# A one-core decoder step: queries spread over the partitions by DMA, four PSUM banks for the products, cached pages and value quads moved, squares of two norms added up by VectorE

## What is computed

```
h = x
for i in (0, 1):
    hn = rms_norm(h, g_pre[i])
    out = gla_mixer(hn, ...) if i == 0 else sb_mixer(hn, ..., k_all, v_all, ...)
    h = h + out
    h = h + sigmoid(rms_norm(h, g_ple[i]) @ w_ple_gate[i]) * (p[i] @ w_ple_up[i])
    if i == 0:
        k_new, v_new = split(rms_norm(h, g_kv) @ w_kv)
        k_all = concat(cache_k[page_table], k_new)      # 16 pages of 128 positions for each sample
        v_all = concat(cache_v[page_table], v_new)
return rms_norm(h, g_final), states, k_new, v_new
# stick breaking: A[t,s] = sigmoid(z_ts) * prod_{s<j<t} (1 - sigmoid(z_tj)), z = q.k/sqrt(64) + bias_h
```

## Time and profile before

| | |
|---|---|
| runs | 950.82, 952.33, 953.08 us, median 952.33 |
| profiled execution | 954.14 us, span 951.2 us between its first and last instruction |
| busy in the span | PE 892.9, DVE 549.9, ACT 439.4, POOL 293.6 us |
| moved by DMA | 228.26 MB, 240 GB/s over the span |

### The profile page before, as it was taken

The page is one execution under the profiler, slowest core; times in us unless marked ns, Lnnn a source line. Parts: engine busy times, 40 slices in busy tenths (PEclk is TensorE's granted clock), DMA queues, the critical chain, the costliest instruction groups (busy, mean ns, idle before and its releaser), DMA issues.

```text
span 951.2 us, 14940 instructions
## 1 busy us (share of the span) xinstructions
PE 892.9 (94%) x5205; PEld 622.0 (65%) x5205; DVE 549.9 (58%) x676; ACT 439.4 (46%) x1369; POOL 293.6 (31%) x157
## 2 busy tenths in 40 slices
PE   5899999999999999999897989999989999899995
PEld 3656677777754444544366877887755455599994
DVE  4454396878846848776888351222257867554553
ACT  5502472324466565657543331222157767343533
POOL 3000004943427966778996000000000000021110
PEclk9989999999999999999998999999999999999998
DMA  9898976743359858779998209989889879232202
GB/s 316 287 374 288 369 231 215 256 156 114 120 200 378 274 204 285 261 258 349 340 330 271 85 23 318 362 290 345 311 289 324 300 257 366 95 95 84 89 1 90
DMA packets 108090, 228.26 MB, mean 240 GB/s; under 512 B 7249, under 2 KB 66232, under 8 KB 108016
## 3 DMA queue, kind: packets, MB, share of 16 engines
q1 hardware_dynamic: 49520, 167.41, 48.6%
q10 hardware_dynamic: 58496, 59.90, 19.1%
HBM read 216.18 MB, written 11.11 MB: 239 GB/s over the span
## 4 chain that ended last, share of the span: by engine, by line
PE 64%; DMA 9%; DVE 9%; ACT 9%; issue 4%; POOL 3%; SPq 2%; ACTq 0%; DVEq 0%; POOLq 0%
PE pp L1543 18%; PE pp L1546 13%; PE pp L1961 6%; PE pp L1531 5%; DMA slot<-in_cache_k_dram 4%; ACT slot L771 4%; POOL slot L570 3%; PE pp L1918 3%; DMA s<-in_state_gla_dram 3%; PE pp L1508 2%; PE pp L1528 2%; PE pp L1945 1%; DVE zall L1232 1%; PE pp L1932 1%; PE pp L1623 1%
## 5 line engine op out<-in xcount | busy, mean ns | idle before, releaser
L570 POOL TENSOR_TENSOR slot<-slot,qb 128x1024 f32<-128x1024 f32 x103 | 262.9, 2584 | 130.7 <-DMA slot<-in_cache_k_dram 88.1
L1232 DVE TENSOR_REDUCE zall<-slot 128x16 f32<-128x1024 f32 x103 | 123.9, 1214 | 49.7 <-POOL slot L570 41.2
L1054 DVE TENSOR_TENSOR w_lo<-w_raw,w_hi 128x1024 fp32r<-128x1024 f32 x57 | 78.1, 1371 | 77.1 <-ACT w_hi L622 77.0
L771 ACT ACTIVATE slot<-slot 128x64 f32<-128x64 f32 x400 | 95.6, 240 | 31.1 <-POOL slot L570 31.1
L622 ACT CAST w_hi<-w_raw 128x1024 fp32r<-128x1024 f32 x58 | 60.5, 1044 | 73.5 <-PE pp L1546 21.6
L1531 PE MATMUL pp<-xn,w_unsplit 128*128 128x512 f32 x192 | 84.6, 593 | 2.6 <-DVE q1T L1077 2.6
L1531 PE MATMUL pp<-xn,w_raw 128*128 128x512 f32 x192 | 84.6, 593 | 0.2 <-ACT xn L633 0.2
L1546 PE MATMUL pp<-xa_hi,w_hi 128*128 128x512 f32 x200 | 82.5, 412 | 0.0
L1546 PE MATMUL pp<-xa_hi,w_lo 128*128 128x512 f32 x200 | 79.7, 399 | 0.0
L1543 PE MATMUL pp<-xb_hi,w_hi 128*128 128x260 f32 x384 | 79.3, 288 | 0.0
L1546 PE MATMUL pp<-xa_lo,w_hi 128*128 128x512 f32 x200 | 79.2, 396 | 0.0
(11 more groups left out here) (305 smaller groups left out, 1559.8 us busy)
## 6 DMA issues: line engine op xcount, KB each, us to landing
slot<-in_cache_k_dram SPq DMA_DIRECT2D x128, 512.0 KB, 5.4
slot<-in_cache_v_dram SPq DMA_DIRECT2D x120, 512.0 KB, 5.6
w_raw<-in_gla_w_in_dram ACTq DMA_DIRECT2D x12, 1024.0 KB, 8.2
slot<-in_gla_w_in_dram SPq DMA_DIRECT2D x24, 512.0 KB, 10.9
w_raw<-in_w_kv_dram ACTq DMA_DIRECT2D x8, 1024.0 KB, 10.8
w_raw<-in_w_ple_gate_dram ACTq DMA_DIRECT2D x6, 1024.0 KB, 5.3
s<-in_state_gla_dram SPq DMA_DIRECT2D x1, 4096.0 KB, 28.8
out_dram<-s ACTq DMA_DIRECT2D x4, 1024.0 KB, 8.1
```

The source lines that it names most:

```text
L570: nc.gpsimd.tensor_tensor(slot[s][:], slot[s][:], qb[:, (n // NPG) % 2, :], ALU.mult).then_inc(S("k_mul_pool"), 1)
L771: ins = nc.scalar.activation(part, part, ACT.Copy, accum_out=zall[:, n % NPG, b * SH + h:b * SH + h + 1])
L1054: nc.vector.tensor_tensor(lo, raw, hi.bitcast(F32), ALU.subtract).then_inc(S("w_split"), 1)
L1232: nc.vector.tensor_reduce(zall[:, n % NPG, b * SH:(b + 1) * SH], at.rearrange("p (h d) -> p h d", d=HD), AX.X, ALU.add).then_inc(S("k_used ...
```

## The change

- **Queries by DMA.** `query_everywhere` and `query_out` go from PE and ACT. SP writes `q1L` to a row-wise array in device memory, `q_rows` (4 DMAs of 8 x 256), and then loads row b into all 128 partitions (8 DMAs of 128 x 1024), the first two before page 4, the others at pages 24, 40, 56, 72, 88, 104.
- **Four banks.** From the fourth v tile to the last q1 tile, products go round banks 0 to 3, so PE may be up to four tiles ahead of DVE.
- **Pages.** v has 8 pages in place of 10, g1 8 in place of 6. In q1 POOL multiplies two pages of four, DVE two, and ACT adds up two at every second tile.
- **Norms 1 and 2.** DVE adds each square tile but the last to `sqacc`, element by element (`keep_squares`: 6 TENSOR_TENSORs a norm, of 512 or 520 columns); PE then multiplies `sqacc` and the last square by ones (`norm_squares`), between the sixth and seventh k-tile of the next phase's first product. ACT takes `rms(1)` behind its page, not ahead of it; DVE takes the wait for it behind its pages.
- **g1.** DVE works off pages ahead of the gate's multiplication; the running product stands one tile earlier; the weights go back in two halves, at g1 tiles 6 and 7, in place of all at tile 7.
- **Quads and heads.** `scores(0)` and `sample_features(1)` stand before the last two transposes of V; one quad a head; `sample_features(3)` behind the last `values`; DVE's scans ahead of `sample_gate`.
- Small moves: `split_lo(2)` behind two short DVE steps, `gla_inside(0)` ahead of a wait.

```
-for _name, _c in (("v", (0, 0, 0, 2, 2, 2, 2, 2)), ("g", (2,) * 8), ("wo0", (4,) * 8), ("ple0", (4,) * 8),
-                  ("q1", (4,) * 8), ("g1", (4, 2, 0, 0, 0, 0, 0, 0))):
+for _name, _c in (("v", (0, 0, 0, 0, 2, 2, 2, 2)), ("g", (2,) * 8), ("wo0", (4,) * 8), ("ple0", (4,) * 8),
+                  ("q1", (4,) * 8), ("g1", (4, 4, 0, 0, 0, 0, 0, 0))):
...
 def on_pool(n):
-    return all(n - pages[0] < 3 for pages in map(pages_at, PAGES_THROUGH) if n in pages)
+    return all(n - pages_at(j)[0] < (2 if phase_of(j) == "q1" else 3) for j in PAGES_THROUGH if n in pages_at(j))
...
+def banks_of(j):
+
+    m = tiles_through(j) - 1
+    if wide(j):
+        return (2 * (m % 2), 2 * (m % 2) + 1)
+    return (m % 4,) if m >= FOUR_BANKS else (m % 2,)
...
+            def query_everywhere(b):
+
+                if b >= 2:
+                    n = (b - 1) * NPG
+                    sp.wait_ge(S("k_used"), n - summed_by_act(n))
+                    sp.wait_ge(S("k_mul_pool"), pool_pages(n))
+                sp.dma_start(qb[:, b % 2, :], q_rows[b:b + 1, :].to_broadcast([P, D])).then_inc(S(f"qb_in{b % 2}"), 16)
...
+                if n == 4:
+                    sp.wait_ge(S("s_q1"), 1)
+                    for g in range(GH):
+                        sp.dma_start(q_rows[:, g * HV:(g + 1) * HV], q1L[SW * g:SW * g + NS, :]).then_inc(S("q_row"), 16)
+                    sp.wait_ge(S("q_row"), 16 * GH)
+                    query_everywhere(0)
+                    query_everywhere(1)
+                elif NPG < n < NPAGES - NPG and n % NPG == 8:
+                    query_everywhere(n // NPG + 1)
...
+            def keep_squares(i, k):
+
+                n, t = i * KT + k, NP_TOK if i == 1 else T
+                dve.wait_ge(S("sq"), n + 1)
+                if k == 1:
+                    if i == 2:
+                        dve.wait_ge(S("sq_normed"), 1)
+                    nc.vector.tensor_tensor(sqacc[:, 0:t], work[:, 0, 0:t], work[:, 1, 0:t], ALU.add).then_inc(S("sq_kept"), 2)
+                else:
+                    dve.wait_ge(S("sq_kept"), (KT - 1) * (i - 1) + k)
+                    nc.vector.tensor_tensor(sqacc[:, 0:t], sqacc[:, 0:t], work[:, n % 2, 0:t], ALU.add).then_inc(S("sq_kept"), 1)
...
+            def norm_squares(i):
+
+                n = (i + 1) * KT - 1
+                pe.wait_ge(S("r_root"), i)
+                pe.wait_ge(S("sq_kept"), (KT - 1) * i)
+                pe.wait_ge(S("sq"), n + 1)
+                for sq, flags in ((sqacc, dict(start=True, stop=False)), (work[:, n % 2, :], dict(start=False, stop=True))):
...
-                if i == 7:
-                    for g in range(4):
-                        sample_weights_back(g)
+                if i in (6, 7):
+                    sample_weights_back(2 * i - 12)
+                    sample_weights_back(2 * i - 11)
```

More of the change, by code:

```diff
@@ L159, in on_act, with tiles_before @@
 def on_act(n):
-    return any(len(pages) >= 4 and n == pages[0] for pages in map(pages_at, PAGES_THROUGH))
+    return any(len(pages_at(j)) >= 4 and n in pages_at(j)[:2 if phase_of(j) == "q1" and j % 2 == 0 else 1]
+               for j in PAGES_THROUGH)
 def summed_by_act(n):
     return sum(on_act(i) for i in range(n))
[L169 to L173, removed]
+FOUR_BANKS = PHASES["v"][2] + 3
+def banks_of(j):
[3 more added lines that the diff above has]
+    return (m % 4,) if m >= FOUR_BANKS else (m % 2,)
+def tiles_before(j):
+    return max((tiles_through(i) for i in range(1, j) if set(banks_of(i)) & set(banks_of(j))), default=0)
 QUADS = NPAGES // QUAD
@@ L641, in square @@
                         act.wait_ge(S("sq_added"), (KT - 1) * norm + tile + 1)
+                elif n >= KT + 2:
+                    norm, tile = (n - 2) // KT, (n - 2) % KT
+                    if tile == KT - 1:
+                        act.wait_ge(S("sq_normed"), norm)
+                    else:
+                        act.wait_ge(S("sq_kept"), (KT - 1) * (norm - 1) + tile + 1)
                 elif n >= 2:
@@ L938, in head_sigmoids, with pair_queries @@
                                          bias=biasbc[:, h:h + 1], scale=HD ** -0.5).then_inc(S("sig_p"), 1)
+            def pair_queries(i):
+                if i < 4:
+                    act.wait_ge(S("mm"), last_tile("V") - (1 if i < 2 else 0))
+                else:
+                    act.wait_ge(S("z_p"), len(ZBANKS) * 2 * (i - 3))
+                nc.scalar.copy(qz[i % 4][0:HD, 0, :], q1T[0:HD, i, :])
+                nc.scalar.copy(qz[i % 4][HD:P, 1, :], q1T[HD:P, i, :]).then_inc(S("qz"), 1)
             for i in range(24):
@@ L1626, in token_major @@
                 last.then_inc(done, 1)
-            def query_everywhere(b):
-                if b:
-                    pe.wait_ge(S("qb_in"), b)
-                else:
-                    pe.wait_ge(S("s_q1"), 1)
-                    pe.wait_ge(S("s_sqrt"), 4)
-                for g in range(GH):
-                    last = nc.tensor.matmul(pp[1][:, g // 2, (g % 2) * HV:(g % 2 + 1) * HV],
-                                            ident[:, SW * g + b:SW * g + b + 1].to_broadcast([P, P]), q1L[:],
-                                            start=True, stop=True)
-                last.then_inc(S("qb_mm"), 1)
-            def queries_at(j):
-                for b in range(NS):
-                    if query_job(b) == j:
-                        query_everywhere(b)
             pe.wait_ge(S("xs_in"), 16 * 5)
@@ L1767, in gla_scores @@
                 if h == 0:
+                    gla_inside(h)
                     pe.wait_ge(S("v_out"), 8)
@@ L1775, in gla_scores, with gla_inside @@
                     pe.wait_ge(S("att_out"), h)
+                    gla_inside(h)
+            def gla_inside(h):
                 for b in range(TB):
@@ L1852, in _ @@
                     product(PHASES["wo0"][0] + u, KT)
-                if u:
-                    add_squares(1, u - 1)
-                queries_at(PHASES["wo0"][0] + u)
             up_tile0(0)
+            up_tile0(1)
             for u in range(8):
-                product(PHASES["ple0"][0] + u, 2 * KT, wait_x=(u == 0))
                 if u == 0:
-                    add_squares(1, KT - 1)
-                if u + 1 < KT:
-                    up_tile0(u + 1)
-                if u:
-                    add_squares(2, u - 1)
-                queries_at(PHASES["ple0"][0] + u)
+                    product(PHASES["ple0"][0], 2 * KT, wait_x=True, tiles=range(KT - 2))
+                    norm_squares(1)
+                    product(PHASES["ple0"][0], 2 * KT, wait_x=True, tiles=range(KT - 2, KT))
+                else:
+                    product(PHASES["ple0"][0] + u, 2 * KT)
+                if u >= 2:
+                    up_tile0(u)
             for u in range(8):
-                product(PHASES["q1"][0] + u, 3 * KT, wait_x=(u == 0))
                 if u == 0:
-                    add_squares(2, KT - 1)
-                queries_at(PHASES["q1"][0] + u)
+                    product(PHASES["q1"][0], 3 * KT, wait_x=True, tiles=range(KT - 2))
+                    norm_squares(2)
+                    product(PHASES["q1"][0], 3 * KT, wait_x=True, tiles=range(KT - 2, KT))
+                else:
+                    product(PHASES["q1"][0] + u, 3 * KT)
             def kv_transposes(t):
@@ L1992, in _ @@
                     value_quad(QUAD * (i - 8))
+                if i == 23:
+                    scores(0)
+                    sample_features(1)
                 if i >= KV_LAG + 8:
```

135 lines of the change are left out of this document (60 added, 75 removed).

## The result

The changed kernel takes 936.78 us, the median of 4 runs (936.58 to 939.55), against 952.71 before (950.82 to 954.38, 4 runs). The ratio is 0.984, with a 95% interval of 0.9814 to 0.9866: 15.9 us or 1.6% faster, clear of the noise. The prediction had said 921.0, with a range from 908 to 936. The sign was right, half of the gain is missing, and the time lies just above the range.

The account below looks back on a forecast made before the run. PE was taken to bound most stages, the page path (DVE, ACT, POOL) wo0 to the last key page. Terms 5.2 + 13.3 + 5.6 + 7.3 = 31.4 us gave 921 us, range 908 to 936.

Parts of the forecast that it names:

- Term 1: v and g: three queries leave PE for SP's DMAs, 5.2 us won; bounds 0 and 5.2.
- if POOL's start after the queries holds up a v tile: v: sign of being wrong; POOL's later start was forecast to keep nobody on PE's path waiting.
- Term 2: wo0 to the last key page: priced on the page path of DVE, ACT and POOL, 13.3 us won; bounds 0 and 36.
- wo0 and norm 1: wo0 tiles slower, but no page sum or query copy between 1/root and the first gate: 4.5 us won.
- ple0 (1.8 forecast, -2.4): ple0: seven tiles of 9.46 us fall to the page path's 9.2, 1.8 us won.
- q1 (2.6, -3.3): q1: eight tiles of 7.93 us fall to 7.6, set by DMA, 2.6 us won.
- g1 (3.4, -1.5): g1 to the last page: 23.6 us falls to 20 on DVE, 3.4 us won.
- Term 3: Weights going back in g1: PE's 4.02 us wait and K's slow first tile both go, 5.6 us; bounds 1.5 and 5.6.
- Term 4: Heads: fewer waits by V's last transposes, one quad a head, earlier end, 7.3 us won; bounds 3 and 8.
- The stretch to the last key page gains nothing: Rival for wo0 to the last key page: more DMA and slower wo0 eat term 2's gain; 934, chance 0.25.
- The additions did not cost more than all else: Rival denied here: twelve DVE additions each wait out POOL, costing 30 us; 964, chance 0.04.
- PE did not bound the stretch: Rival denied here: PE bounds everything, so all 36 us of term 2 come; 898, chance 0.12.

Follow-up runs that it names:

- experiment 9: Changed kernel with the page counts of before, ten pages in v and six in g1: 936.31 us, ratio 0.9828.
- experiment 13: Changed kernel with norm squares summed on PE, ACT's page sum ahead in wo0 and ple0, q1's pages three on POOL, one on DVE: 920.09 us.
- experiment 10: Changed kernel with all four groups of sample weights turned back behind g1's last tile again: 940.18 us, ratio 0.9874.

## Why the prediction was half right

- **What bounds the kernel.** That wo0 to g1 goes by the page path and not by PE was right. PE's 30 us less of work brought 15.9, and two banks or four made no difference to the stretch that can be read.
- **Term 1 (5.2).** 8.5 came, and 8.9 if the means of all profiles are taken (284.2 with the kernel before and its variant, 275.3). With the old page counts it is 2.3. So the queries by DMA alone bring less than forecast, because of a wait that I had listed as something that could make me wrong, "if POOL's start after the queries holds up a v tile", and the two pages fewer, which I had given no price there, bring the rest. Of those 6.6 us the trace of experiment 9 shows 3.6 as PE's wait and about 2.5 as the lower clock behind it.
- **Term 2 (13.3) is the step that failed**; it came out at -2.8. Its first part, wo0 and norm 1, was right by its sum (4.3 against 4.5), by the order on ACT as described. The others were priced as work per tile ("the page path asks for 6.98 + 0.9 and the two additions at 0.6 and 0.7: 9.2"). That counts POOL's and DVE's time and takes the pages as there. They were not: in ple0 POOL waited for DMA 7 times at a DMA share of 0.77, 19.5 us in all, as the earlier trace rows show for the kernel before with 10.53 us, which I read as a bound for another thing. The pace was that of a ring through ACT's slot: with nothing but ACT's order changed the stretch fell by 5.4 us here and by 5.3 on the kernel before. The ring is old, so it says why the stages had nothing to give; what made them slower is what the change put beside it. Undone one at a time, the additions gave 5.2 us of stretch, the six loads 3.5, the two pages more in g1 5.1 (3.0 of them in g1 itself), and the new sharing 3.1; these overlap, so their sum of 17 is only near the 16 that were missing, and how the 16 divide among them is not shown.
- **ple0 (1.8 forecast, -2.4)**: the additions at 0.6 or 0.7 were 0.68 to 2.85, 1.4 in the mean of the six there. **q1 (2.6, -3.3)**: I took DMA to 1.0 at 360 GB/s; it ran at 332, share 0.90, and q1 reached no more than 348 and 0.96, in experiment 13 with the old sharing. The 6.5 us a tile for POOL and DVE counted 0.9 for each page that DVE multiplies; these took 1.96 in the mean of 15, up to 3.25, and DVE was busy 55.1 of 64 us. **g1 (3.4, -1.5)**: "That there are two pages more is paid by the wait for the gate's table and sigmoid" was wrong: g1 took 25.1 us with eight pages and 22.1 with six, in two pairs of kernels. The other moves there won 1.5.
- **Term 3 (5.6).** 4.8 in the trace, of which experiment 10 gives back 2.0. The wait was real, and so was the fallen clock, 0.50 behind 4.02 us of waiting; behind 2.41 us it did not fall. What brought the other 2.8 was not tested alone.
- **Term 4 (7.3).** 5.4 in the trace, not tested alone.
- **The rivals.** "The stretch to the last key page gains nothing", 934 with a chance of 0.25, is near what happened, and both reasons given for it, the loads and the slower wo0, had their share (wo0 to its last residual 54.8 to 57.8). Outside the stretch 18.7 us came against 18.1 forecast. That this is so near is in part luck: term 1's gain came in good part from the two pages, which had no price, and only 2.0 of term 3's 4.8 are shown to be its own. The additions did not cost more than all else. PE did not bound the stretch.

The Trainium skill (SBUF — State Buffer, Who interferes with whom) says that GpSimd and a DVE instruction with two SBUF inputs lock one shared port for a whole instruction. The trace agrees: an addition takes 0.69 us alone and 2.85 beside POOL, which is 0.69 and 2.16 more, nearly a whole multiplication of 2.33.

## What to carry over

A stage that is "bound by a path" has to be priced as a ring, if its buffers come back through the same engines: follow one slot from its release to its next release, and count the waits in order beside the busy time of each engine. Look for the consumer that frees a slot last although it could do so first; moving ACT's page sum ahead of a wait cost nothing and brought 6 to 10 us, on both kernels. And price a side job on an engine in the state that the other edits aim at, since the additions on DVE cost nearly twice as much once the pages flowed (9.8 us against 5.2).

## What the runs showed of the chip

- The same DVE addition of 512 or 520 columns took between 0.69 and 2.85 us, and its median rose from 0.99 to 1.92 us when nothing but ACT's order was changed.
- A load of one query row into 128 partitions, 0.52 MB, stands in SP's queue like a key page: it took 7.1 us to land in the median, and cost 0.6 us of the stretch.
- With next to nothing changed before it, wo0 began anywhere from 273.4 to 277.5 us in ten profiles. All ten have a wait of PE of 2.1 to 2.5 us near 190. In four the granted clock was 0.50 for 3.4 us there; these began at 275.5 to 277.5, the other six at 273.4 to 275.4. Why it fell in some was not looked for.
- A wait of PE can cost more than itself: behind 3.62 us of waiting in experiment 9 the granted clock was 0.50 until 171.4, and matmuls that took 0.40 us took 0.63.
